# A transformer block's first output projection with features on partitions, with the router's logits, the residual and the norm taken from its blocks

## What is computed

```
mod = silu(c) @ w_ada + b_ada              # six vectors of 1024
sh_m, sc_m, gt_m, sh_f, sc_f, gt_f = split(mod, 6)
h   = modulate(rmsnorm(x, norm_mix_g), sh_m, sc_m)
...                                        # attention and pooling of h @ w_in
mix = concat(attn_out, pool_out) @ w_out
x1  = x + gt_m * mix
h   = rmsnorm(x1, norm_ffn_g) * (1 + sc_f) + sh_f
logits = h @ [w_router_group | w_router_expert] + bias      # 4 + 32 columns
...                                        # top group, its top 2 experts, 32 SwiGLU experts
x2  = x1 + gt_f * ffn
```

## Time and profile before

| | |
|---|---|
| median of 3 executions | 883.09 us (881.92 to 885.6) |
| the profiled execution, its own time | 885.27 us |
| span of the profiled execution | 883.5 us |
| TensorE, busy share of the span | 84% |
| VectorE, ScalarE, GpSimd | 42%, 33%, 17% |
| mean rate of all transfers | 238 GB/s (of HBM reads) |
| chain that ended last | PE 62%, DMA 19%, DVE 10%, ACT 5% |

### The profile page before, as it was taken

The page is one execution under the profiler, slowest core; times in us unless marked ns, Lnnn a source line. Parts: engine busy times, 40 slices in busy tenths (PEclk is TensorE's granted clock), DMA queues, the critical chain, the costliest instruction groups (busy, mean ns, idle before and its releaser), DMA issues.

```text
span 883.5 us, 11281 instructions
## 1 busy us (share of the span) xinstructions
PE 740.7 (84%) x4630; PEld 558.8 (63%) x4630; DVE 368.0 (42%) x527; ACT 294.1 (33%) x400; POOL 146.7 (17%) x105
## 2 busy tenths in 40 slices
PE   4889989789766775667798799689878799999996
PEld 2776646664212322122797798689766799999995
DVE  2344550551001010102775868724653564455353
ACT  3343331222001100003446334416643354444431
POOL 0002222000000000003029640100122223222220
PEclk9789998869869887888899999989889799999999
DMA  9789756398999999999335513312321525435501
GB/s 364 309 320 359 289 193 237 148 424 363 421 423 421 421 421 421 421 420 387 144 138 191 191 34 158 119 73 96 143 80 64 215 112 223 181 153 203 186 41 48
DMA packets 31432, 211.01 MB, mean 239 GB/s; under 512 B 4752, under 2 KB 5008, under 8 KB 6544
## 3 DMA queue, kind: packets, MB, share of 16 engines
q1 hardware_dynamic: 31376, 210.23, 60.0%
HBM read 209.17 MB, written 1.05 MB: 238 GB/s over the span
## 4 chain that ended last, share of the span: by engine, by line
PE 62%; DMA 19%; DVE 10%; ACT 5%; issue 3%; SPq 1%; ACTq 0%; DVEq 0%
PE psum L403 61%; DMA raw<-in_w_exp 17%; DVE wlo L465 2%; ACT whi L451 2%; DMA raw<-in_w_ada 2%; PE psum L411 1%; DVE xn L1745 1%; DVE XT L551 1%; DVE XL L563 0%; DVE Pr L1861 0%; DVE XL L1816 0%; DVE xn L1779 0%; DVE xn L1856 0%; DVE X L853 0%; DVE XT L868 0%
## 5 line engine op out<-in xcount | busy, mean ns | idle before, releaser
L465 POOL TENSOR_TENSOR wlo<-raw,whi 128x2048 fp32r<-128x2048 f32 x21 | 98.5, 4693 | 681.5 <-ACT whi L451 681.5
L403 PE MATMUL psum<-XH,whi 128*128 128x256 f32 x672 | 197.4, 294 | 15.1 <-DVE XL L563 6.9
L403 PE MATMUL psum<-XL,whi 128*128 128x256 f32 x672 | 195.1, 290 | 0.0
L403 PE MATMUL psum<-XH,wlo 128*128 128x256 f32 x672 | 194.3, 289 | 0.0
L465 DVE TENSOR_TENSOR wlo<-raw,whi 128x2048 fp32r<-128x2048 f32 x53 | 140.9, 2682 | 62.7 <-ACT whi L451 62.7
L451 ACT ACTIVATE whi<-raw 128x2048 fp32r<-128x2048 f32 x74 | 138.5, 1905 | 58.9 <-PE psum L403 33.8
L403 PEld LDWEIGHTS psum<-XH,whi 128*128 128x128 f32 x672 | 132.7, 198 | 16.9 <-DVE XL L563 7.6
L403 PEld LDWEIGHTS psum<-XL,whi 128*128 128x128 f32 x672 | 132.5, 197 | 0.3
L403 PEld LDWEIGHTS psum<-XH,wlo 128*128 128x128 f32 x672 | 132.5, 197 | 0.0
L403 PE MATMUL psum<-raw,G 128*32 128x512 f32 x512 | 71.7, 710 | 26.8 <-DMA raw<-in_w_exp 26.8
L403 PEld LDWEIGHTS psum<-raw,G 128*32 128x32 f32 x512 | 18.6, 127 | 75.7 <-issue 75.1
(11 more groups left out here) (282 smaller groups left out, 956.2 us busy)
## 6 DMA issues: line engine op xcount, KB each, us to landing
raw<-in_w_exp SPq DMA_DIRECT2D x96, 1024.0 KB, 25.3
raw<-in_w_ff SPq DMA_DIRECT2D x32, 1024.0 KB, 4.8
raw<-in_w_ada SPq DMA_DIRECT2D x24, 1024.0 KB, 7.1
raw<-in_w_in SPq DMA_DIRECT2D x22, 1024.0 KB, 5.4
raw<-in_w_in_t SPq DMA_DIRECT2D x8, 1024.0 KB, 7.0
raw<-in_w_out_t SPq DMA_DIRECT2D x4, 1024.0 KB, 6.5
raw<-in_w_out SPq DMA_DIRECT2D x4, 1024.0 KB, 4.8
raw<-in_w_o_hg SPq DMA_DIRECT2D x2, 1024.0 KB, 5.0
```

The costliest lines, as they stand in the source:

```text
L403: return e.matmul(o, l, r, start=start, stop=stop, skip_group_check=True)
L465: e.tensor_tensor(wlo[j % NS][:, :], ring[slot[i]], whi[j % NS][:, :], ALU.subtract).then_inc(*steps_(("lo", j), ("freed", i)))
```

## The change

The projection is turned: for each of eight blocks n of 128 features, 128 columns of `w_out` are stationary and the 256 tokens of `XH`/`XL` are moved, 12 matmuls for each half of the contraction. x itself is transposed beforehand by TensorE (`pe_turn(..., "x0")`) and copied by ACT to `XT` (`act_xt`), and gt_m becomes columns, so that x1 of a block is one VectorE instruction. Behind it TensorE takes the block's part of the logits (`pe_logits`) with `WS`, which is `WR` times the norm's columns, and turns the block back into banks 4 to 7 (`pe_back`). The shift's part of the logits comes from eight matmuls (`shift`), once; the norm's factor rs is applied to the logits and to the gathered rows afterwards. The products for gt_f (modulation blocks 10 and 11) move from TensorE to VectorE (`dve_products`). `SEL` becomes 16x8, broadcast in the matmul. The small loads of `WR`, `RB` go to SP's early list, the load of the final norm's row (into the tile that now holds `WR`, `WS`, `RB`, `RS`) behind `mask`.

```diff
@@ pieces of w_ada for gt_f, on VectorE (new)
+        def dve_products(e, b):
+            s = acc[b % 2]
+            e.wait_ge(*at(("accread", b - 2)))
+            for k in range(2):
+                i = ai[(b, k)]
+                r = ring[slot[i]]
+                e.wait_ge(*landed(i))
+                for c in range(4):
+                    x, m = r[:, 512 * c:512 * c + 512], cact[:, 4 * k + c:4 * k + c + 1]
+                    if k + c == 0:
+                        x = e.tensor_scalar(s[:, :], x, m, None, ALU.mult)
+                    else:
+                        e.wait_ge(*ada_dve.last())
+                        x = e.scalar_tensor_tensor(out=s[:, :], in0=x, scalar=m, in1=s[:, :], op0=ALU.mult, op1=ALU.add)
...
@@ sp_mixer
-            sp_small(e, "gtm", GTM, a["b_ada"][0:1, 2048:3072].broadcast_to([128, 1024]))
+            sp_small(e, "wr", WR, a["w_router"])
+            sp_small(e, "rb", RB, a["b_router"][0:1, :].broadcast_to([128, 36]))
@@ act_mixer
+            act_xt(e, (0, 1))
             act_ada(e, 7)
+            act_xt(e, (2, 3))
...
-            act_ada(e, 10)
-            act_ada(e, 11)
@@ dve_mixer
-            for b in range(8, 12):
-                dve_ada(e, b)
-            for t in range(2):
-                for b in range(2):
-                    cs = slice(512 * b, 512 * b + 512)
-                    d, p = xn[:, t, cs], ps[2 * b + t]
-                    e.wait_ge(*at(("mix_sum", t, b)))
-                    e.tensor_tensor(d, p[:, :], GTM[:, cs], ALU.mult).then_inc(*mix_dve(("read", ("mixed_out", t, b))))
-                    e.wait_ge(*mix_dve.last())
-                    e.tensor_tensor(X[:, t, cs], X[:, t, cs], d, ALU.add).then_inc(*mix_dve(("x1", t, b)))
+            dve_ada(e, 8)
+            dve_ada(e, 9)
+            e.wait_ge(*mix_dve.last())
+            e.scalar_tensor_tensor(out=AF, in0=mcol[:, 4, :], scalar=1.0, in1=gcol[:, 1, :], op0=ALU.add, op1=ALU.mult).then_inc(
+                *mix_dve("AF"))
+            e.wait_ge(*mix_dve.last())
+            e.wait_ge(*loaded("wr"))
+            e.tensor_tensor(WS, WR, b3(AF, 36), ALU.mult).then_inc(*mix_dve("WS"))
+            e.wait_ge(*at("shifted"))
+            e.wait_ge(*loaded("rb"))
+            e.tensor_tensor(RS, bank("shift")[:, 0:36], RB, ALU.add).then_inc(*mix_dve(("read", "shift"), "RS"))
+            dve_products(e, 10)
+            dve_products(e, 11)
+            for n in range(8):
+                e.wait_ge(*at(("mix_sum", n)))
+                e.wait_ge(*at(("x0", "T", n // 2)))
+                e.scalar_tensor_tensor(out=XT[:, n, :], in0=ps[n % 4][:, 256 * (n // 4):256 * (n // 4) + 256],
+                                       scalar=mcol[:, 2, n:n + 1], in1=XT[:, n, :], op0=ALU.mult, op1=ALU.add).then_inc(
+                    *mix_dve(("x1", n), ("read", ("x1", n))))
@@ pe_mixer
             pe_ada(e, vb, 5)
+            pe_turn(e, vb, X, 0, mix_pe, "x0")
+            pe_turn(e, vb, X, 1, mix_pe, "x0")
             token_half(e, ab, 6, 0, "u", 1)
...
             pe_block(e, vb, 7)
+            pe_turn(e, vb, X, 2, mix_pe, "x0")
+            pe_turn(e, vb, X, 3, mix_pe, "x0")
...
+            for n in range(4):
+                pe_mix_part(e, n, 1)
+            pe_ada(e, rest, 9)
+            for n in range(4, 8):
+                pe_mix_part(e, n, 1)
+            p = rest.take(e, "shift")
+            e.wait_ge(*at(("mod", 7)))
+            e.wait_ge(*loaded("wr"))
+            for c in range(8):
+                i = mm(e, p[:, 0:36], BF[:, c:c + 1].broadcast_to([128, 128]), WR[:, c, :], c == 0, c == 7)
+            i.then_inc(*mix_pe("shifted"))
+            for n in range(8):
+                pe_mix_part(e, n, 0)
+                if n == 6:
+                    for c in range(4):
+                        pe_logits(e, c)
+                if n == 7:
+                    pe_logits(e, 4)
+                if n >= 2:
+                    pe_back(e, n - 2)
+            pe_logits(e, 5)
+            pe_logits(e, 6)
+            pe_back(e, 6)
+            pe_back(e, 7)
+            pe_logits(e, 7)
+            for k in range(1, 4):
+                holder[k] = ("x1", 4 + k)
+            for b in (10, 11):
+                pe_ada(e, Banks([b - 9]), b)
@@ pe_mix_part(e, n, kb), new waits
+            if not kb and b:
+                e.wait_ge(*at(("x1", k)))
@@ new functions
+        def pe_back(e, n):
+            e.wait_ge(*at(("x1", n)))
+            for t in range(2):
...
+                i = mm(e, ps[k][:, 128 * (n % 4):128 * (n % 4) + 128], XT[:, n, 128 * t:128 * t + 128], C["ident"], n % 4 == 0, False)
+            i.then_inc(*mix_pe(("back", n)))
+        def pe_logits(e, n):
+            if n == 0:
+                e.wait_ge(*at(("x1", 4)))
+                e.wait_ge(*at("WS"))
...
+            e.wait_ge(*at(("x1", n)))
+            for t in range(2):
+                i = mm(e, bank("route")[:, 36 * t:36 * t + 36], XT[:, n, 128 * t:128 * t + 128], WS[:, n, :], n + t == 0, n == 7)
+            i.then_inc(*mix_pe(("routed", n)))
+        X1 = [("routed", 7), ("x1", 7)]
@@ sp_moe
-            sp_small(e, "wr", WR[:, :, :], a["w_router"])
-            sp_small(e, "rb", RB[:, :], a["b_router"][0:1, :].broadcast_to([128, 36]))
+            sp_load(e, E0 + 15)
+            e.wait_ge(*at("mask"))
@@ act_moe
-            for t in range(2):
-                e.wait_ge(*at(("scored", 3) if t == 0 else ("accread", 11)))
-                act_stat(e, t, at(("x1", t, 1)), moe_act, "n2")
...
-            e.activation(XNH[:, :, :], ym[:, :, :], ACT.Copy).then_inc(*moe_act("xnh"))
+            for h in range(2):
+                e.wait_ge(*at(("back", 4 * h + 3)))
+                for t in range(2):
+                    e.activation(flat(G[0][:, 4 * t + 2 * h:4 * t + 2 * h + 2, :]), ps[4 + 2 * t + h][:, :], ACT.Square,
+                                 accum_out=(ss, ss2)[h][:, t:t + 1]).then_inc(*moe_act(("n2sq", h)))
...
+            for t in range(2):
+                for h in range(2):
+                    e.activation(XNH[:, t, 512 * h:512 * h + 512], ps[4 + 2 * t + h][:, :], ACT.Copy, scale=rs[:, t:t + 1]).then_inc(
+                        *moe_act(("xnh", 2 * t + h)))
@@ dve_moe: the scaling, the columns and the old XNL go; two sums come
+            e.tensor_tensor(ss[:, :], ss[:, :], ss2[:, :], ALU.add).then_inc(*rt_dve("ss"))
             dve_route(e)
...
             dve_spread(e, 0)
+            dve_ada(e, 10)
+            dve_ada(e, 11)
@@ dve_route: RL, and XNL behind mask
-            e.tensor_tensor(RL[:, :, :], bank("route")[:, 0:72].rearrange("p (a b) -> p a b", a=2), row2(RB[:, :]), ALU.add).then_inc(
+            for t in range(2):
+                e.scalar_tensor_tensor(out=RL[:, t, :], in0=bank("route")[:, 36 * t:36 * t + 36], scalar=rs[:, t:t + 1], in1=RS,
...
+            for t in range(2):
+                for h in range(2):
+                    e.scalar_tensor_tensor(out=XNL[:, t, cs], in0=ps[4 + 2 * t + h][:, :], scalar=rs[:, t:t + 1], in1=XNH[:, t, cs],
@@ pe_moe: four transposition groups, 16 logit products and the copy of X into banks 4 to 7 go
-            for q in range(4):
-                pe_turn(e, banks, ym, q, moe_pe, "n2")
...
```

More of the change, by code:

```diff
@@ L183, in build @@
         FR = t1("FR", [16, 384], fr)
+        SEL = t1("SEL", [16, 8], fr)
         one = t1("one", [128, 128], fr)
@@ L189, in build @@
         p1.close()
+        WR, WS = [GTM[:, 288 * i:288 * i + 288].rearrange("p (a b) -> p a b", a=8) for i in range(2)]
+        RB, RS = GTM[:, 576:612], GTM[:, 612:648]
         p2 = ExitStack()
@@ L346, in build @@
         raw_landed = [sem(f"raw_landed{i}") for i in range(len(ring))]
-        small = {n: sem(f"ld_{n}") for n in ("c", "first", "cst", "later", "badc", "g", "x", "wf", "bfg", "bands", "pw", "psc", "gtm", "gtf",
+        small = {n: sem(f"ld_{n}") for n in ("c", "first", "cst", "later", "badc", "g", "x", "wf", "bfg", "bands", "pw", "psc", "gtf",
                                              "fin", "wr", "rb", "lb", "bg", "hng", "fg")}
@@ L735, in act_soft, with act_xt @@
                              accum_out=sms[:, h, t:t + 1]).then_inc(*mix_act(*[("soft", h), ("read", ("sc", h))] if t else []))
+        def act_xt(e, qs):
+            for q in qs:
+                e.wait_ge(*at(("x0", "turned", q)))
+                if q == 0:
+                    e.wait_ge(*at("flog_sum"))
+                e.activation(flat(XT[:, 2 * q:2 * q + 2, :]), bank(("x0", q))[:, :], ACT.Copy).then_inc(
+                    *mix_act(("read", ("x0", q)), ("x0", "T", q)))
         def act_band(e, g):
@@ L1071, in pe_mix_part @@
                 e.wait_ge(*at(("cat", 4 * kb + c)))
[L1072 to L1075, removed]
-        X1 = [("x1", t, b) for t in range(2) for b in range(2)] + [("wread", 11)]
+                w = slice(512 * c + 128 * k, 512 * c + 128 * k + 128)
@@ new lines, in pe_mix_part @@
```

(27 more changed lines are left out.)

96 lines of the change are left out of this document (35 added, 61 removed).

## The result

The changed kernel takes 893.27 us (median of 7 executions, 886.38 to 895.01), the kernel before in the same comparison 883.85 us. The ratio is 1.0098 with a 95% interval of 1.0060 to 1.0137: slower by 9.4 us in the medians. Five of the seven executions lie between 893.09 and 895.01 us, the other two at 886.38 and 887.78. The profiled execution took 895.01 us at a span of 893.2.

What follows compares the result with a forecast made beforehand. The prediction took the expert weights' stream, by its start and holes, as the bound. X1's shift +14.5, small loads -1.7 and the hole -2.6 gave +10.2 us on 883.09: 893 us, range 886 to 902.

Steps and rivals of the forecast that it cites:

- The step that decides: VectorE's products stand behind its wait for the shift and ahead of x1(0), leaving TensorE idle 8.4 us at pe_back(0).
- X1: Moment the expert weights' loads can first go out: 169.92 us before, forecast 184.4 us, +14.5 us.
- Bound: Expert stage: ends when its weight stream's last byte lands, so the stream's start and its holes count.
- Behind X1: From X1 to the first gate-and-up: 17.2 us instead of 27.8; worth -1.7 us for loads and -2.6 for the hole.
- The hole: Expert stream, 198 to 204 us: queues wait for ring slots; claimed to close, -2.6 us.
- Ahead of the projection: Transposes of x, narrower modulation sums and bank waits on a busy TensorE: +3.1 us, projection starting at 137.4 us.
- Products: VectorE's 16 operations for modulation blocks 10 and 11, 14 of them at an interpolated 0.75 us: 12.0 us.
- The wait: TensorE at pe_back(0) stands idle for x1(0) from 158.6 to 167.0 us: 8.4 us.
- Behind the wait: TensorE's remaining blocks, logit products and turning back x1: 14.4 us, plus 3.0 us for the low clock.
- Half-rate products: Rival at VectorE's products: 14 operations take 1.28 us each; +17.6 us, 901 us; chance 4%.
- A clock that stays low: Rival on TensorE after its idling: clock at 0.50 until X1; +21.6 us, 905 us; chance 13%.
- TensorE as the bound: Rival at pe_back(0): products ready by 158.6 us, no TensorE stall; -1.2 us, 882 us; 7% faster, 12% no change.

Runs made afterwards that it cites:

- early ring: Eight expert pieces issued ahead of SP's wait for the logits; on the changed kernel 888.28 us, ratio 1.0053 to the kernel before; also added to other runs.
- the wait filled: Changed kernel with 66 unread matmuls of 256 columns where TensorE waits for VectorE's products: 889.17 us, ratio 1.0065 to the kernel before.
- products early: Changed kernel with VectorE's 16 products for modulation blocks 10 and 11 ahead of its wait for the shift: 881.96 us, ratio 0.9978 to the kernel before.

## Why the prediction was right

Forecast 893.2 us, measured 893.27; +10.2 against +9.4 us. The step that decides stood as written: VectorE's list puts the products between the shift and x1(0), TensorE stands at pe_back(0), and everything queues behind. (883.09 + 10.2 is 893.3; the forecast was written 0.1 short.) That the time agrees to 0.1 us is luck: the changed kernel's executions spread over 8.6 us, X1 came out at 184.5 us as forecast (184.4) because the projection started 1.3 us later than I had it and the part behind the wait was 1.2 us shorter, and the kernel before took 0.8 us more in this comparison than the median that I had added to. Point by point:

- **Bound.** The end follows the stream. In the seven profiles in which the stream starts behind the logits (the changed kernel among them) the last expert weights are in 232.3 to 232.7 us after its first issue. In the other seven, the kernel before and the six runs with an early ring, they are in 206.1 to 206.6 us after the slots' return. The end is the later of the two; in the changed kernel they are 1.4 us apart (417.2 and 415.8 us). The spans show the same more coarsely, 705 to 709 and 681 to 683 us more, because what follows the stream took 472 to 476 us.
- **Behind X1.** -4.3 forecast, -4.9 measured: span less X1 went from 713.6 to 708.7 us. The hole and the router loads' bytes, booked at 3.0, were worth 3.6: from the first stream issue to the last weights 236.3 us before, 232.7 after. But it was closer than I thought: first gate-and-up 17.2 us behind X1 by the forecast, 21.0 in fact. I had listed the two sums as work for TensorE that hides in a wait, and had not followed their PSUM banks: the second gather needs bank 2, which VectorE empties late in its list. With sum 11 in bank 3 the whole stretch took 17.1 us, so the bank is what cost the 3.8. By the two rules above the slots may come back 26 us behind the stream's start; they did after 25.0, so the hole closed with 1.4 us to spare, where my 21.2 would have left 5. (The row in question gives a share of 0.58, so the hole is 2.5, not 2.6 us by that reckoning.)
- **Ahead of the projection.** +3.1 forecast, +4.4 in the profile. The mechanism was right (with the transposes elsewhere the projection starts at 133.5 us). The size can't be told more closely: in seven profiled executions with the same list ahead of it, the projection started at 135.6, 135.7, 137.1, 138.2, 138.3, 138.7, 139.5 us and in the kernel before twice at 134.3. The mean of the seven is 137.6, +3.2. Part of that spread is the clock (last section); where the rest comes from is open.
- **Products.** 12.0 us forecast; 155.87 to 167.8 us. The interpolated 0.75 us for the unseen form is what it takes (0.752). The rule of the Trainium skill (Vector Engine (DVE) Microarchitecture Reference, "Points that are easy to get wrong") that it runs at half throughput with two SBUF sources that aren't bf16 is not borne out by these 14 rows either, which take 0.752 us beside 0.692 for a tensor_tensor of the same size.
- **The wait.** 8.4 forecast, 8.25 measured.
- **Behind the wait.** 17.4 forecast, 16.2 measured. The term that was off is the clock: 3.0 us booked. With the wait filled the same work takes 14.5 us (167.7 to 182.2), where I had 14.4, so the clock costs 1.7: I had six or seven slow microseconds, and the clock was back after 3.7.
- **The rivals.** Half-rate products: no. A clock that stays low: no; in the four profiles with this wait it was back at 1.00 some 3 to 6 us after the wait's end, within the blocks of the projection and the first turned-back ones. TensorE as the bound: that is nearly what the kernel becomes when the products are early (the median is 1.9 us under the kernel before; I had -1.2 for it).

## What to carry to other kernels

A piece of work that is free for an engine is not free for its list: put what nobody waits for where the engine would wait anyway, ahead of the wait and not behind it. Two lines moved were worth 11 us here. When a stage is bound by a stream into a ring, two moments count, the start of the stream and the return of the first slots; shortening the chain to the first use pays only if the ring is full by then, and small loads that the chain needs must be issued ahead of the bulk. And for every tile or bank that moved work touches, look who takes it next and when it is read.

## What the runs showed of the hardware

TensorE's granted clock can fall while the engine is busy all but without a gap. Two executions of the same list in this stretch (columns as in rows 2):

```profile
88.00:95.00 7.00, 6.89 (x34) 5.34 (x34) 2.76 (x11) 3.52 (x9) 1.82 (x2) 0.76 0.86 359
```

```profile
88.00:95.00 7.00, 6.68 (x41) 4.84 (x44) 4.32 (x12) 3.87 (x10) 1.83 (x2) 1.00 0.99 414
```

The first is the changed kernel, the second the run with the products early, which reaches the same instructions 1.05 us later. In both, the four narrow float32 matmuls of a modulation sum (from 88.73 and 89.78 us) are followed by a dense block of 12 matmuls, and TensorE has no marked wait from 78 us to the block's end. In the first the clock was low for part of the block (PEclk 0.76; TensorE busy 6.89 of 7 us), and the block took 4.4 us; in the second the clock stayed at 1.00 and it took 2.9. The projection began later in the first by 0.5 us.

The same holds behind a short wait. Ahead of the projection TensorE waits 2.15 us for VectorE's `dT` in every one of the seven profiles with this list. Behind it, the changed kernel and the run with sum 11 in bank 3:

```profile
136.00:140.00 4.00, 4.00 (x22) 3.48 (x19) 1.44 (x5) 2.49 (x3) 1.16 (x1) 0.50 0.75 305
```

```profile
136.00:140.00 4.00, 4.00 (x36) 4.00 (x35) 0.80 (x3) 1.92 (x2) 2.26 (x1) 1.00 0.45 184
```

The seven reach the end of that wait within 2.0 us of each other (131.9 to 133.9) and the projection within 3.8 us (135.6 to 139.5): the clock behind the wait adds the difference. A single profile of such a kernel can be off by 2 us either way.
